# Ten hidden strips by plain products in two passes, in place of eight: a two-layer attention and feed-forward kernel

## The chip, the cores and the metric

One core of a Trainium2 chip runs the whole program in one launch. The metric is the device time in microseconds (us), lower is better. Before the change: 2373.8 us, the median of three runs (2369.51 to 2375.25).

## The reference, cut to what matters

Two attention layers, a pooling mixer and a gated feed-forward block work on 1024 tokens of width 1024, all in float32. The change is in the feed-forward block at the end:

```
def conv_ffn(x, w_in, conv_w, conv_b, w_out):          # x: 1024 tokens x 1024
    h = causal_depthwise_conv(x @ w_in, conv_w, conv_b)  # w_in: 1024 x 5632, 3 taps along the tokens
    val, gate = jnp.split(h, 2, axis=-1)                 # 2816 hidden columns each
    return (jax.nn.silu(gate) * val) @ w_out             # w_out: 2816 x 1024
```

The 2816 hidden columns are 22 strips of 128. The hidden tensor is called u below. It never lies whole on the chip's memory: it goes to DRAM (`ud`) and is fetched for the last matrix product.

## The kernel before, in words

Each factor of a float32 product is split into a high and a low part, so one 128x128 by 128x512 block takes three matmuls (high-high, high-low, low-high). The instructions of all engines come from one list, `steps`: the planner puts steps into it, and each engine's program walks the list in order and issues what is its own. So an engine that waits in one step holds back all of its later steps.

Two ways make the strips of u.

**Plain products by token halves.** `half_task` (line 1475 on) makes one *half*: one strip's value or gate columns for 512 tokens, 8 row tiles x 3 = 24 matmuls into one bank of PSUM (`ffn mm`, lines 1937 to 1939, where a helper records them). `odd_last` (from line 1571) lists the halves: first all strips 0 to 7 for tokens 0 to 511 (the first pass, 16 halves, order `FIRST_PASS`), then all for tokens 512 to 1023 (the second pass, 16 halves, order `SECOND_PASS`). I number the halves 0 to 31 here. After its matmuls a half is left by ScalarE (`half leave`, through the helper of line 2187: the last tap and the bias; in the first pass it also keeps two columns in `TAIL`, in the second it adds them to the first two tokens in three tiny activations) and VectorE adds two taps from PSUM (`half conv`, lines 2749 and 2751). Its bank is free when line 2751 is done. A gate half is then put through silu on ScalarE and multiplied with the value half on VectorE (line 2757). The bank of a half is this:

```
p.bank = (4, 6, 2, 0)[half_no[0] % (3 if n == 0 else 4)]
```

So the first pass goes round three banks and the second, with `half_no` counting on, round four. Strip `TWICE` (6) is last in the first pass and first in the second; its 8 split weight pieces are kept and used again, and `ahead` splits no further than that allows while its first use runs. All other weights are loaded and split for each pass: a piece is 128x256, its high part is made by ScalarE (line 2187), its low part by GpSimd (line 2853); in the second pass every fourth low part goes to VectorE (line 2466). A piece is split 9 pieces ahead of its use, a half uses 4.

One iteration of the planner puts a quarter of a half (one piece, 6 matmuls), then the steps that were deferred from earlier halves, then one step of a side chain. Beside the first pass the side chain is the pooling mixer and the norm of the second token half (`mixed(1)`), and then `turn_sums` (lines 2764, 2770, 2775 on VectorE, with ScalarE's `turn hi`): 28 iterations that make the sums and their splits of the whole normalised input that the block products need. In the kernel before they begin in the first quarter of half 14.

In the second pass the two strips of a pair are brought together (`half_pair`, `pair_sums`): the first-pass results come back from DRAM and VectorE makes four sums (line 2781) in three tiles of X, stored again. The tiles alternate:

```
u.tiles = ((0, 4, 1), (5, 2, 6))[(len(x_parts) - 1) % 2]
```

**Block products.** A unit makes two strips by seven products of blocks each for value and gate together (`product`, lines 2176 to 2178, 12 matmuls of 128x512 each, so 168 for a unit). Their sums of weights (2792), splits of weights (2187, 2786), the adding up of products (2801), taps over 1024 tokens (2807, 2809) and gating (2815) are on VectorE and ScalarE. The first post of a unit goes into tile 0 of X, the second into tile 2. Before the change the 14 remaining strips take 7 units. Six more units of block products make the last matrix product out of u, in three groups of hidden strips (0 to 7, 8 to 15, 16 to 21), and the result is stored. `start_products` is called four halves before the end of the second pass.

Of the kernel before, what the change touches and what calls it, by code (L numbers as in the profile page):

```python
# [27 lines left out]
MEM_UNITS, MEM_RAW = 32, 7  # L28
B_S, B_PT, B_O, B_X = 2, 4, 6, 7
Y_BANKS, X_BANKS, Z_BANKS = ((1, 3), (5, 7)), (4, 6), (2, 0)  # L30
PLAIN = 8
TWICE = 6
FIRST_PASS, SECOND_PASS = (0, 1, 2, 3, 4, 5, 7, 6), (6, 7, 0, 1, 2, 3, 4, 5)
GROUPS = ((0, 4), (8, 4), (16, 3))
A11, A12, A21, A22, ADD = range(5)
SPLIT_OF = (A11, A12, A11, ADD, A21, A12, A22)
# [159 lines left out]
def build(nc, d):  # L196
    ctx = ExitStack()
    with ctx:
        def sb(name, shape, dt=F):
            return ctx.enter_context(nc.sbuf_tensor(name, shape, dt))  # L200
# [27 lines left out]
        SM = sb("SM", [128, 16])  # L228
        SN = sb("SN", [128, 16])
        PSB = sb("PSB", [128, 8])  # L230
        TAIL = sb("TAIL", [128, 16, 2])
        CARRY = sb("CARRY", [128, 8])
        PS = ctx.enter_context(nc.psum_tensor("PS", [128, 8, 512], F))

# [137 lines left out]
        def add_units(us):  # L372
            first, tiles = len(subs), []
            for pieces, kn, n in us:
                per = 256 // n if n <= 256 else 1
                for k in range(0, kn, per):
                    m = min(per, kn - k)
                    subs.append((len(units), k * n, m * n))
                    tiles.append(m)
                units.append(pieces)  # L380
            return first, tiles
# [32 lines left out]
        def ahead(i):  # L414
            while at["split"] < min(i + NSPL - 1 + (4 if at["deep"] else 0), len(subs)):
                no = at["split"]
                split_place(no)
                u = subs[no][0]
                while at["load"] <= min(u + (MEM_RAW if at["load"] < MEM_UNITS else NRAW) - 1, len(units) - 1):
                    load_next()  # L420
                s_whi.add()
                if no < at["both"]:
                    on = s_wlov if no % (2 if no < 2 * MEM_UNITS else 3) else s_wlop
                else:
                    on = s_wlov if at["second"] and no >= at["second"] and no % 4 == 3 else s_wlop
                half_lo.append((on, on.add()))
                put("split", no)
                at["split"] += 1
# [500 lines left out]
        def in_units(w, cols):  # L929
            return [w_cols(w, 0, 4, cols), w_cols(w, 4, 4, cols)]  # L930
# [508 lines left out]
        def pool_task(n, g):  # L1439
            u = pool_first[n, g] = add_units([w_cols(d["pool_w"][g], 0, 2, [(0, 256)])])[0]  # L1440

            def later(c, px):
                yield
                yield
                yield
                yield
                square(ffn[n], c, px)
                squared[n] += 1
                if n == 1:
                    yield  # L1450
                    kept[c] = (d_xt[c], d_xt[c].add(16))
                    put("x spill", c, px)

            def gen():
                ahead(u)
                for o in range(2):
                    c = 2 * g + o
                    bank = at["bank"] % 2
                    at["bank"] += 1
                    pool_no[n, c] = s_pm.add()  # L1460
                    if o == 1:
                        used[u] = used[u + 1] = (s_pm, s_pm.n)
                    put("pool mm", n, g, o, u, bank, s_px.add())
                    defer(later(c, (s_px, s_px.n)))
                    if o == 0:
                        yield
            tasks.append((f"pool{n}{g}", gen, 2))
# [7 lines left out]
        def half_task(j, base, n):  # L1475
            if n == 1 and j == TWICE:
                p = Ffn(j, base, n, *twice[base])
            else:
                p = Ffn(j, base, n, *add_units(in_units(d["ffn_in"], [(base + 128 * j, 128)])))
            if n == 0 and j == TWICE:  # L1480
                twice[base] = (p.first, p.tiles)
# [33 lines left out]
            def gen():  # L1515
# [3 lines left out]
                for i in range(len(p.tiles)):  # L1519
                    ahead(min(p.first + i, twice[0][0] + 1) if n == 0 and j == TWICE else p.first + i)  # L1520
                    if i == len(p.tiles) - 1:
# [49 lines left out]
        def odd_last(first_rest, second_out):  # L1571
            for oc in range(8):
                first_rest(oc)
            for oc in range(8):
                second_out(oc)
                if 2 <= oc < 6:
                    pool_task(0, oc - 2)
            for i in range(2 * PLAIN):
                half_task(FIRST_PASS[i // 2], HID * (i % 2), 0)
                if i in (4, 6, 8, 9):  # L1580
                    pool_task(1, (4, 6, 8, 9).index(i))
            at["second"] = len(subs)
            for i in range(2 * PLAIN):
                half_task(SECOND_PASS[i // 2], HID * (i % 2), 1)

        units_of = [[Quad("in", PLAIN + 2 * u + x, None, u, x) for x in (0, 1)] for u in range((HT_TILES - PLAIN) // 2)]
        for group in GROUPS:
# [4 lines left out]
        for no, p in enumerate(run):  # L1592
            p.no = no
        entered = (HT_TILES - PLAIN) // 2
        wanted = [(m, which) for unit in units_of for m, which in
# [587 lines left out]
        def scalar_program(e):  # L2183
            w = Waits(e)

            def act(out, in_, func=ACT.Copy, **more):
                return e.activation(out, in_, func, **more)  # L2187
# [9 lines left out]
            for kind, *of in steps:  # L2197
# [166 lines left out]
                elif kind == "half leave":  # L2364
# [6 lines left out]
                    if n == 0:  # L2371
                        act(TAIL[:, p.at, :], ps[:, 510:512]).then_inc(s_fa.sem, 1)
                    act(T, ps, ACT.Identity, bias=COL[:, C_CB + col:C_CB + col + 1],
                        scale=COL[:, C_CW + 4 * HT_TILES + col:C_CW + 4 * HT_TILES + col + 1]).then_inc(s_fa.sem, 1)
                    if n == 1:
                        w0, w1 = COL[:, C_CW + col:C_CW + col + 1], COL[:, C_CW + 2 * HT_TILES + col:C_CW + 2 * HT_TILES + col + 1]
                        t0, t1 = TAIL[:, p.at, 0:1], TAIL[:, p.at, 1:2]
                        w.wait_ge(s_fa, p.left - 3)
# [744 lines left out]
```

## Time and profile before, and how to read it

| | |
|---|---|
| median of three runs | 2373.8 us |
| the profiled execution's own time | 2380.02 us |
| its span on the core | 2378.2 us |
| TensorE matmul busy | 2284.0 us, 96% |
| VectorE busy | 1611.1 us, 68% |
| ScalarE busy | 1312.1 us, 55% |
| GpSimd busy | 686.5 us, 29% |
| mean granted TensorE clock | 0.989 |

Engines: PE is TensorE, PEld its weight load, DVE VectorE, ACT ScalarE, POOL GpSimd. A matmul's record covers its whole passage, and the next one starts before it ends, so the rate is read from starts or from counts in a window. On the time axis of the trace the first pass ends at about 1793 us, the second runs from 1801 to 1892, the 7 units of block products for the strips from 1892 to about 2160, and the last matrix product until the end.

### The profile page before, as it was taken

To read this page: it belongs to the slowest core of one execution; us is meant where nothing else is said; L and a number is where in the kernel's file an instruction comes from. 1 tells how busy PE (TensorE), PEld (TensorE's weight loads), DVE (VectorE), ACT (ScalarE), POOL (GpSimd) and SP (SyncE) were. 2 spreads that over 40 slices of the span, in tenths; PEclk is the share of its full clock that TensorE was granted. 3 is DMA by queue.
4 is the path that set the end of the run, shared out by engine and by line. 5 is a ranking of instruction groups with operands and counts; after the bars stand their busy time and mean duration, and the time that the engine had idled before them with its cause. 6 is when DMAs were issued, how large, how long until landed. Compare 5 with 4: busy or idle time off the path is not lost. (4 is left out here: it accounts for less than half of the span.)

```text
span 2378.2 us, 35378 instructions
## 1 busy us (share of the span) xinstructions
PE 2284.0 (96%) x11782; PEld 1939.8 (82%) x11782; DVE 1611.1 (68%) x3297; ACT 1312.1 (55%) x3022; POOL 686.5 (29%) x843
## 2 busy tenths in 40 slices
PE   7999999999999999999999999898998999999999
PEld 6888788888887878888888888786777888887887
DVE  7444676677886433346655566668789788889787
ACT  6444566566775434456656556655555645455532
POOL 3454332311245542222222222555562300000000
PEclk9999999999999999999999999999999999999999
DMA  7322101111243342323232233532352633345734
GB/s 225 117 72 67 40 24 32 32 34 47 61 125 108 94 132 64 93 67 94 85 93 87 77 93 94 188 89 75 88 170 71 201 105 111 113 141 177 229 110 139
DMA packets 331203, 241.68 MB, mean 102 GB/s; under 512 B 66320, under 2 KB 284688, under 8 KB 330512
## 3 DMA queue, kind: packets, MB, share of 16 engines
q1 hardware_dynamic: 331024, 239.42, 33.1%
q8 instruction: 96, 1.57, 0.3%
q14 instruction: 83, 0.68, 0.1%
HBM read 195.59 MB, written 43.78 MB: 101 GB/s over the span
## 5 line engine op out<-in xcount | busy, mean ns | idle before, releaser
L2853 POOL TENSOR_TENSOR WS<-WR,WS 128x256 fp32r<-128x256 f32 x635 | 494.4, 798 | 1027.0 <-ACT WS L2187 1025.0
L1937 PE MATMUL PS<-HT,WS 128*128 128x512 f32 x1492 | 605.6, 406 | 23.5 <-POOL WS L2853 6.5
L1939 PE MATMUL PS<-HT,WS 128*128 128x512 f32 x1492 | 585.9, 393 | 0.0
L1938 PE MATMUL PS<-HT,WS 128*128 128x512 f32 x1492 | 584.6, 392 | 0.0
L1937 PEld LDWEIGHTS PS<-HT,WS 128*128 128x128 f32 x1492 | 282.9, 190 | 83.9 <-issue 15.1
L1939 PEld LDWEIGHTS PS<-HT,WS 128*128 128x128 f32 x1492 | 282.1, 189 | 62.1
L1938 PEld LDWEIGHTS PS<-HT,WS 128*128 128x128 f32 x1492 | 283.5, 190 | 52.2
L2187 ACT ACTIVATE PT<-PS 128x512 fp32r<-128x512 f32 x352 | 185.7, 528 | 208.5 <-PE PS L2050 208.2
L2187 ACT ACTIVATE WS<-WR 128x256 fp32r<-128x256 f32 x658 | 245.7, 410 | 89.2 <-PE PS L1939 61.8
L2435 DVE TENSOR_TENSOR PT<-PS,PT 128x512 fp32r<-128x512 f32 x352 | 211.4, 609 | 94.0 <-ACT PT L2187 91.6
L2083 PE MATMUL PS<-PT,QKV 128*128 128x256 f32 (+1 forms) x1248 | 209.3, 289 | 3.2 <-DVE YB L2614 2.4
L2187 ACT ACTIVATE QKV<-PS 64x512 fp32r<-64x512 f32 (+2 forms) x208 | 121.6, 585 | 140.5 <-PE PS L1939 122.0
L2083 PEld LDWEIGHTS PS<-PT,QKV 128*128 128x128 f32 x1248 | 180.5, 192 | 10.5 <-ACT PT L2187 3.8
L2050 PE MATMUL PS<-ID,PY 128*128 128x128 f32 x1072 | 184.1, 275 | 0.1
L2436 DVE SCALAR_TENSOR_TENSOR QKV<-PS,QKV 64x512 fp32r<-64x512 f32 (+1 forms) x112 | 77.2, 689 | 113.8 <-ACT QKV L2187 111.6
L2187 ACT ACTIVATE PY<-PY,ST 128x384 f32<-128x384 f32 (+1 forms) x192 | 115.6, 602 | 37.5 <-DVE ST L2565 25.5
L2037 PE MATMUL PS<-QKV 128*128 128x384 f32 (+2 forms) x320 | 121.7, 381 | 14.5 <-ACT PY L2187 13.0
L2558 DVE CUSTOM_DVE_ANT_0 PY<-PS,EO 128x384 f32<-128x384 f32 (+1 forms) x192 | 103.5, 539 | 42.3 <-PE PS L2038 41.6
L2050 PEld LDWEIGHTS PS<-ID,PY 128*128 128x128 f32 x1072 | 128.1, 141 | 0.6 <-ACT PY L2187 0.4
L2435 DVE TENSOR_TENSOR QKV<-PS,QKV 64x512 fp32r<-64x512 f32 (+2 forms) x96 | 63.9, 666 | 93.6 <-ACT QKV L2187 92.3
L2545 DVE TENSOR_REDUCE ST<-PS 128x1 f32<-128x256 f32 (+1 forms) x128 | 102.3, 819 | 35.9 <-PE PS L2025 20.9
L2187 ACT ACTIVATE HT<-EO 128x512 fp32r<-128x512 f32 x112 | 70.1, 628 | 93.1 <-PE PS L2178 30.1
(286 smaller groups left out, 4594.8 us busy)
## 6 DMA issues: line engine op xcount, KB each, us to landing
WR<-in_w_in_odd SPq DMA_DIRECT2D x106, 256.0 KB, 2.9
EO<-in_grid SPq DMA_DIRECT2D x48, 384.0 KB, 3.1
WR<-in_ffn_in SPq DMA_DIRECT2D x60, 256.0 KB, 2.9
WR<-in_w_in_even SPq DMA_DIRECT2D x100, 128.0 KB, 2.6
WR<-in_w_out_odd SPq DMA_DIRECT2D x48, 256.0 KB, 2.8
yd<-PY SPq DMA_DIRECT2D x44, 256.0 KB, 3.3
EO<-in_ffn_in SPq DMA_DIRECT2D x35, 256.0 KB, 3.1
WR<-in_w_in_even SPq DMA_DIRECT2D x34, 256.0 KB, 2.9
```

What stands on the lines that cost most here:

```text
L1937: e.matmul(out, wh, rh, start=start, stop=False)
L1938: e.matmul(out, wh, rl, start=False, stop=False)
L1939: return e.matmul(out, wl, rh, start=False, stop=stop)
L2037: e.matmul(out, q, kh, start=True, stop=False)
L2050: m = e.transpose(PS[:, B_PT + pb, o + 128 * z:o + 128 * z + 128], p_at(job.c, job.scores[x].slot, p0, p0 + 128), ID[:, :])
L2083: m = e.matmul(out, vv, p, start=a, stop=b)
L2187: return e.activation(out, in_, func, **more)
L2435: return e.tensor_tensor(out, src, f32(hi), ALU.subtract)
L2436: return e.scalar_tensor_tensor(out=out, in0=src, scalar=scale, in1=f32(hi), op0=ALU.mult, op1=ALU.subtract)
L2545: e.tensor_reduce(st[:, 1:2], src, AX.XY, ALU.max, negate=True).then_inc(s_mx.sem, 1)
L2558: e.tensor_tensor_reduce(out=two_parts(p, s.cut), in0=src, in1=two_parts(bias, s.cut), scale=1.0, scalar=NEG, op0=ALU.add, op1=ALU.max, ac ...
L2853: e.tensor_tensor(ws(i, 1, n), RAW[raw_slot(u)][:, o:o + n], f32(ws(i, 0, n)), ALU.subtract).then_inc(s_wlop.sem, 1)
```

## The change

The number of plain strips goes from 8 to 10, the strip with kept weights from 6 to 8, the two orders get two more strips, and `TAIL` gets 20 rows. Nothing else is edited. So the passes have 20 halves each (0 to 39), six units of block products make the remaining 12 strips, and every position that is counted from the start of the first pass (the pooling products after its entries 4, 6, 8, 9; the side chain) stays where it was.

```
-PLAIN = 8
-TWICE = 6
-FIRST_PASS, SECOND_PASS = (0, 1, 2, 3, 4, 5, 7, 6), (6, 7, 0, 1, 2, 3, 4, 5)
+PLAIN = 10
+TWICE = 8
+FIRST_PASS, SECOND_PASS = (0, 1, 2, 3, 4, 5, 6, 7, 9, 8), (8, 9, 0, 1, 2, 3, 4, 5, 6, 7)
...
-        TAIL = sb("TAIL", [128, 16, 2])
+        TAIL = sb("TAIL", [128, 2 * PLAIN, 2])
```

## Rows read from the trace of the kernel before

**Rows 1.** Windows: length, then busy (x instructions) of PE, PEld, DVE, ACT, POOL; clock; DMA.

```profile
1640.00:1800.00 160.00, 146.75 (x646) 119.30 (x644) 130.36 (x188) 84.37 (x191) 89.23 (x97) 0.96 0.37 117
...
1812.00:1843.00 31.00, 31.00 (x138) 25.47 (x137) 30.69 (x45) 19.48 (x48) 12.89 (x15) 1.00 0.29 85
...
1847.30:1891.80 44.50, 44.50 (x197) 36.75 (x197) 30.24 (x43) 28.70 (x74) 17.75 (x22) 1.00 0.81 246
1892.00:2154.00 262.00, 261.33 (x1152) 215.88 (x1152) 224.85 (x302) 137.44 (x211) 0.00 (x0) 1.00 0.37 116
1910.00:2150.00 240.00, 240.00 (x1060) 198.82 (x1059) 203.32 (x267) 127.28 (x191) 0.00 (x0) 1.00 0.37 116
```

**Rows 2.** Waits of PE, 1600 to 1910 us: total us, times, longest.

```profile
PE PS L1937 <- DVE SG L2751: 7.7, 1, 7.7
...
PE PS L1937 <- DVE PT L2466: 0.7, 1, 0.7
PE PS L2176 <- ACT X L2187: 0.7, 1, 0.7
```

**Rows 3.** Timeline of PE: start us, us, engine, line; idle before and releaser.

```profile
1792.96 0.39 PE L1939 MATMUL PS<-HT,WS 128*128 128x512 f32 x1
1801.02 0.80 PE L1937 MATMUL PS<-HT,PT 128*128 128x512 f32 x1 [7.67 <-DVE SG L2751]
1801.61 0.63 PE L1938 MATMUL PS<-HT,PT 128*128 128x512 f32 x1
...
1807.04 0.40 PE L1939 MATMUL PS<-HT,WS 128*128 128x512 f32 x1
```

**Rows 4.** Timeline of DVE: the taps of halves 14 to 19.

```profile
1795.11 0.75 DVE L2751 SCALAR_TENSOR_TENSOR SG<-PS,COL,SG 128x510 f32<-128x510 f32 x1
...
1800.22 0.75 DVE L2751 SCALAR_TENSOR_TENSOR SG<-PS,COL,SG 128x510 f32<-128x510 f32 x1
...
1811.36 0.75 DVE L2749 SCALAR_TENSOR_TENSOR PY<-PS,COL,PY 128x511 f32<-128x511 f32 x1 [3.50 <-ACT PY L2187]
...
1818.23 0.75 DVE L2751 SCALAR_TENSOR_TENSOR PY<-PS,COL,PY 128x510 f32<-128x510 f32 x1
...
1826.75 0.75 DVE L2751 SCALAR_TENSOR_TENSOR SG<-PS,COL,SG 128x510 f32<-128x510 f32 x1
...
1833.33 0.75 DVE L2751 SCALAR_TENSOR_TENSOR SG<-PS,COL,SG 128x510 f32<-128x510 f32 x1
```

**Rows 5.** Groups of DVE: the first from 1789.6 to 1801, the others 1812 to 1843.

```profile
L2770 DVE TENSOR_TENSOR EO<-EO 128x512 f32<-128x512 f32 x4 | 2.8, 688 | 0.1
...
L2775 DVE TENSOR_TENSOR QKV<-PY,QKV 128x512 fp32r<-128x512 f32 x6 | 4.5, 772 | 0.0
L2770 DVE TENSOR_TENSOR PY<-PY 128x512 f32<-128x512 f32 x5 | 4.0, 802 | 0.1
L2775 DVE TENSOR_TENSOR QKV<-EO,QKV 128x512 fp32r<-128x512 f32 x4 | 3.5, 904 | 0.0
...
L2466 DVE TENSOR_TENSOR WS<-WR,WS 128x256 fp32r<-128x256 f32 x3 | 1.2, 415 | 0.0
...
L2757 DVE TENSOR_TENSOR SG<-SG 128x512 f32<-128x512 f32 x1 | 1.2, 1225 | 0.0
L2757 DVE TENSOR_TENSOR PY<-PY 128x512 f32<-128x512 f32 x1 | 1.2, 1223 | 0.0
```

**Rows 6.** Timeline of POOL around the end of the first pass.

```profile
1787.41 1.44 POOL L2853 TENSOR_TENSOR PT<-WR,PT 128x256 fp32r<-128x256 f32 x2 [0.28 <-ACT PT L2187]
1804.54 1.17 POOL L2853 TENSOR_TENSOR PT<-WR,PT 128x256 fp32r<-128x256 f32 x1 [15.70 <-ACT PT L2187]
```

**Rows 7.** Timeline of ACT where the block products begin.

```profile
1902.90 0.57 ACT L2187 ACTIVATE X<-PS 128x512 f32<-128x512 f32 x1
...
1906.00 0.60 ACT L2187 ACTIVATE X<-PS 128x512 f32<-128x512 f32 x1 [2.01 <-DMA ud<-X]
```

**Rows 8.** Timeline of DVE there: the last sum of the last plain pair.

```profile
1903.60 0.69 DVE L2781 TENSOR_TENSOR X<-X 128x512 f32<-128x512 f32 x1
```

## The prediction

> **What bounds the kernel now.** I read the windows first. The profile's mean would call TensorE the bound, but the stages differ. In the block products it takes a matmul every 240 / 1060 = 0.226 us with no idle time, and VectorE has 37 us of 240 to spare; in the second pass it takes one every 44.5 / 197 = 0.226 us, with VectorE at 30.24 of 44.5. From 1640 to 1800 us TensorE fits in 646 instructions where 160 us would hold some 700, and from 1812 to 1843 us VectorE is busy for 30.69 of 31 us [rows 1]. So matmuls are the price wherever VectorE keeps up, and around the change from the first pass to the second VectorE sets the pace.
>
> Then the waits of TensorE: between 1600 and 1910 us one wait is the longest, 7.7 us on line 2751, the taps that free a bank [rows 2]. The timeline shows its place: the last matmul of half 15 starts at 1792.96, the first of half 16 at 1801.02; and then the clock: steps of 0.427 us from 1801.61 until 1807.04, 13 of them, where 0.227 is usual, so it ran at 1.2 GHz instead of 2.4 after 7.67 us of idleness [rows 3]. Half 15 has bank 15 mod 3 = 0, half 16 bank 16 mod 4 = 0 of the same list: half 16 waits for its direct predecessor's taps, which end at 1800.22 + 0.75 = 1800.97 [rows 4].
>
> **Matmuls.** The change adds 8 halves, 8 x 24 = 192 matmuls, and removes one unit of 168. Net 24 x 0.227 = **+5.4 us**, on the path, as both stages run at the matmul rate [rows 1].
>
> **The stall between the passes.** The first pass now ends with half 19 (bank 19 mod 3 = 1, bank 6), and half 20 takes bank 4, last used by half 18. There is one half of 5.45 us in between, which looks like the end of the stall. But the 28 steps of turn sums still begin at half 14, so they now all fall beside first-pass halves, and the taps of half 18 queue behind some 20 of them. When are these done? Before, they ended at 1826.75 + 0.75 = 1827.5 [rows 4]. Take away what had delayed VectorE there: 3.50 us in which it waited for half 16 [rows 4], and three low parts of line 2466, each 0.41 long and about 0.33 from start to start [rows 5], which only the second pass has. That gives 1823.0. TensorE without a stall ends half 19 at 1793.2 + 4 x 5.45 = 1815.0 and then waits 8.0 us: the same stall, one half later in relation to its bank, because four more halves let VectorE fall back further. With 2.85 us for the slow clock (13 x 0.2, and 0.25 for the first step) half 21 starts at 1823.0 + 5.45 + 2.85 = 1831.3; before it was at 1801.02 + 5 x 5.45 + 2.85 = 1831.1. Half 21 needs bank 6, free when half 19's taps end, (1833.33 + 0.75) - 3.50 - 4 x 0.33 = 1829.3: no second wait. Term: **+0.2 us**.
>
> **GpSimd beside the sums.** While the kept strip ran, GpSimd had nothing: 15.70 us idle before 1804.54 [rows 6]. Now strips 7 and 9 follow half 14 and their weights go on being split. By the planner's rule of 9 pieces ahead, 16 low parts come to GpSimd before the taps of half 18 are put, where it had 7. VectorE's operations with two inputs in SBUF take 688 ns while GpSimd is idle; with 15 GpSimd instructions about [rows 1] they take 772, 802 and 904 ns on average and 1.22 us singly. The excess is 6 x 0.084 + 5 x 0.114 + 4 x 0.216 + 2 x 0.54 = 3.0 us, 0.2 for each GpSimd instruction [rows 5]. Nine more: **+1.8 us**, at the place where VectorE has no slack. Bounds: 0, if they fall beside operations that read PSUM, to 9 x 0.54 = 4.9.
>
> A rule of the Trainium skill speaks here against the change. "SBUF — State Buffer", section "SBUF: two separate sides", says that VectorE with two SBUF inputs and GpSimd lock one port pair for a whole instruction, and the other blocks. The doubled durations agree; full blocking each time would put the sum near the upper bound.
>
> **Smaller edits.** The wait of 0.7 us on line 2466 in the second pass [rows 2] came from VectorE's arrears; the sums will be over before: **-0.7 us** (bounds -0.7 and 0). The last plain pair is now the fifth, so its sums lie in tiles 0, 4, 1 instead of 5, 2, 6. The unit's first post writes tile 0. It began at 1902.90 [rows 7] and must now follow the pair's last sum, over at 1903.60 + 0.69 = 1904.29 [rows 8]: +1.4, and the next product's wait for the store of tile 2 (2.01 us of ScalarE [rows 7]) goes, which gives back 0.3. **+1.1 us** (bounds 0 and 3, if tile 1's store comes late, though its post is six products off). What TensorE waited there already, 0.7 [rows 2], stays.
>
> At nothing: eight more halves' taps, silu and products on VectorE and ScalarE (VectorE 68% busy in the second pass [rows 1]; in the first they are the queue costed above); 16 weight loads of 256 KB more against 8 fewer, two pairs of stores and fetches more, all on SyncE's queue, with the DMA engines at 0.81 but no wait of TensorE in that stretch [rows 1]. If that cover failed, TensorE would wait for pieces. ScalarE's splits now stand behind turn steps that wait for VectorE; the piece is 9 quarters, 12 us, ahead, and up to 8 us of such waiting vanish in the stall at half 20 anyway.
>
> **Sum:** 5.4 + 0.2 + 1.8 - 0.7 + 1.1 = +7.8 us. The profiled execution's own time, 2380.02, would become 2387.8; it stands 6.2 above the median of the runs, and on the median 2373.8 the forecast is **2381.6 us**, +0.33%. The measurement can tell about 0.3%, 7.1 us, so this lies just past it.
>
> **The rivals.** *The lag is absorbed* (the other side). If VectorE ends half 18's taps by 1815.0, bank 4 is free in time, no stall and no slow clock: 5.4 - (8.06 - 0.23 + 2.85 = 10.7) - 0.7 + 1.1 = -4.9, 2368.9. For it: nothing waits for a direct predecessor any more. Against: 8 us of VectorE work would have to vanish, and it is shown back to back [rows 1, 4]. Chance 0.17, a third of it past -7.1 with some luck elsewhere.
> *GpSimd costs nothing*: the forecast without 1.8, +6.0, 2379.8. VectorE's operations of lines 2764 and 2751 read PSUM and were not lengthened. Chance 0.2, mostly within 0.3%.
> *Full collisions*: every added low part doubles an operation, 4.9 in place of 1.8: +10.9, 2384.7. Chance 0.12. That is the skill's rule with bad luck.
> *Weights late*: pieces for halves 14 to 19 come more than 8 us late, or a fetch holds a pair, 4 us on top: 2386. Against: no wait of TensorE is for a load [rows 2]. Chance 0.06.
> The forecast has 0.45, itself uncertain by 2.5 us: 2379 to 2384, two thirds of it slower.
>
> **Numbers.** Slower: 0.30 + 0.05 + 0.12 + 0.05 = 0.52. Faster: 0.06, and 0.02 for what I don't see, 0.08. Within 0.3%: 0.40. The range reaches from 2370, near the absorbed lag, to 2387, past the late weights.
>
> **What would show it.** Matmuls: 1152 fewer by 168 in the block stage, 8 x 24 more before. Stall: TensorE's longest wait still on line 2751, 7 to 11 us, before half 20, with slow steps after it; if it is under 2 us I am wrong and the lag was absorbed. GpSimd: idle time of some 15 us moved behind half 17, and lines 2770 and 2775 longer beside halves 14 to 17. Tiles: the wait before the fifth block product near 2 us, released by the post into X. The forecast is wrong if VectorE shows gaps between the taps of halves 16 and 18.

## The result, and the profile after

The changed kernel takes 2379.11 us (median of 12 runs, 2376.58 to 2385.75), the one before beside it 2373.28 (12 runs, 2369.51 to 2380.11): ratio 1.003, 95% interval 1.0019 to 1.0040, so 0.3% slower. Run once more against the kernel before (`ten_again` below) the ratio was 1.0014, interval 1.0001 to 1.0027. The two together say slower by 0.14 to 0.3%, some 3 to 7 us. The forecast was 2381.6, +0.33%.

The first part of the page of the kernel after:

```profile
span 2383.8 us, 35528 instructions
## 1 busy us (share of the span) xinstructions
PE 2287.6 (96%) x11806; PEld 1943.3 (82%) x11806; DVE 1598.9 (67%) x3283; ACT 1316.3 (55%) x3054; POOL 705.8 (30%) x871
```

TensorE has 11806 matmuls where it had 11782: 24 more, as counted, while VectorE has less to do than before (1611.1 us then). Where TensorE sets the pace, these extra matmuls are a cost that no schedule hides.

The spans of single executions are a poor measure here, so I set a common point: the transposes of line 2132, which prepare the turn sums in the first quarter ahead of half 14. Up to it both programs issue the same instructions. TensorE's timeline of the kernel before at this point, at the first matmuls of half 21, of the block products and of the last matrix product, and at the last matmul:

```profile
1781.85 0.38 PE L2132 MATMUL PS<-ID,SN 128*128 128x128 f32 x2
...
1831.12 0.39 PE L1937 MATMUL PS<-HT,PT 128*128 128x512 f32 x1
...
1892.05 0.39 PE L2176 MATMUL PS<-HT,WS 128*128 128x512 f32 x1
...
2164.25 0.39 PE L2176 MATMUL PS<-HT 128*128 128x512 f32 x1
...
2374.66 0.39 PE L2178 MATMUL PS<-QKV,WS 128*128 128x512 f32 x1
```

The same places in the kernel after:

```profile
1783.93 0.27 PE L2132 MATMUL PS<-ID,SN 128*128 128x128 f32 x1
...
1833.50 0.39 PE L1937 MATMUL PS<-HT,PT 128*128 128x512 f32 x1
...
1936.86 0.39 PE L2176 MATMUL PS<-HT,WS 128*128 128x512 f32 x1
...
2169.26 0.39 PE L2176 MATMUL PS<-HT,WS 128*128 128x512 f32 x1
...
2380.24 0.39 PE L2178 MATMUL PS<-QKV,HT 128*128 128x512 f32 x1
```

| from | to | before, us | after, us | difference |
|---|---|---|---|---|
| common point | half 21 | 49.27 | 49.57 | +0.3 |
| half 21 | block products | 60.93 | 103.36 | +42.4 |
| block products | last matrix product | 272.20 | 232.40 | -39.8 |
| last matrix product | last matmul | 210.41 | 210.98 | +0.6 |
| common point | last matmul | 592.81 | 596.31 | +3.5 |

The other 2.1 us of the difference between the two spans lie ahead of the common point. Two of the rows hold a piece of chance that cancels in the sum: after a wait of 2.62 us just before the last matrix product, matmuls came at the half rate in this profile of before and not in that of after. This makes the third difference 0.5 us more negative and the fourth 0.6 us more positive; from that wait to the last matmul it is 217.54 us before and 217.56 after.

The waits of TensorE in the kernel after, 1785 to 1936 us, answer to [rows 2]:

```profile
PE PS L1937 <- DVE SG L2751: 6.5, 1, 6.5
PE PS L1937 <- POOL PT L2853: 1.4, 2, 0.8
PE PS L1937 <- DVE PY L2751: 0.4, 1, 0.4
```

The wait of line 2466 and the one at the entry of the block products are gone; the one on line 2751 is there again. Its place in TensorE's timeline, against [rows 3]:

```profile
1819.44 0.39 PE L1939 MATMUL PS<-HT,WS 128*128 128x512 f32 x1
1826.31 0.80 PE L1937 MATMUL PS<-HT,WS 128*128 128x512 f32 x1 [6.48 <-DVE SG L2751]
1826.90 0.63 PE L1938 MATMUL PS<-HT,WS 128*128 128x512 f32 x1
...
1829.85 0.39 PE L1939 MATMUL PS<-HT,WS 128*128 128x512 f32 x1
```

The taps that released it are those of half 18, as the timeline of VectorE shows (against [rows 4]):

```profile
1825.51 0.75 DVE L2751 SCALAR_TENSOR_TENSOR SG<-PS,COL,SG 128x510 f32<-128x510 f32 x1
```

They end at 1826.26, TensorE goes on at 1826.31. The two windows below are the same stretch, 8 to 42 us after the common point, before and after (columns as in [rows 1]). GpSimd has 16 instructions where it had 7, and VectorE goes from instruction to instruction without a wait:

```profile
1789.80:1823.80 34.00, 26.33 (x104) 21.25 (x103) 30.12 (x45) 15.76 (x35) 6.36 (x7) 0.85 0.18 54
```

```profile
1791.90:1825.90 34.00, 26.13 (x112) 20.35 (x110) 33.58 (x47) 17.36 (x41) 12.75 (x16) 0.96 0.29 89
```

### The profile page after: what moved, and what is told of

It reads as the page before. It is cut to its first block and busy times, and to the rows that moved or that the text cites. A ratio compares the mean times of both kernels' runs of the same rounds, so it can differ in the third digit from the quotient of the medians.

```text
span 2383.8 us, 35528 instructions
## 1 busy us (share of the span) xinstructions
PE 2287.6 (96%) x11806; PEld 1943.3 (82%) x11806; DVE 1598.9 (67%) x3283; ACT 1316.3 (55%) x3054; POOL 705.8 (30%) x871
## 5 line engine op out<-in xcount | busy, mean ns | idle before, releaser
L2853 POOL TENSOR_TENSOR WS<-WR,WS 128x256 fp32r<-128x256 f32 x652 | 506.2, 796 | 1051.9 <-ACT WS L2187 1050.8
L1937 PE MATMUL PS<-HT,WS 128*128 128x512 f32 x1528 | 619.0, 405 | 29.7 <-DVE SG L2751 6.5
L1939 PE MATMUL PS<-HT,WS 128*128 128x512 f32 x1528 | 600.0, 393 | 0.0
L1938 PE MATMUL PS<-HT,WS 128*128 128x512 f32 x1528 | 598.6, 392 | 0.0
L1937 PEld LDWEIGHTS PS<-HT,WS 128*128 128x128 f32 x1528 | 289.5, 189 | 91.2 <-issue 12.0
L1939 PEld LDWEIGHTS PS<-HT,WS 128*128 128x128 f32 x1528 | 288.8, 189 | 63.4
L1938 PEld LDWEIGHTS PS<-HT,WS 128*128 128x128 f32 x1528 | 289.9, 190 | 53.6
L2187 ACT ACTIVATE WS<-WR 128x256 fp32r<-128x256 f32 x678 | 252.9, 409 | 96.0 <-PE PS L1939 62.6
L2037 PE MATMUL PS<-QKV 128*128 128x384 f32 (+2 forms) x320 | 122.8, 384 | 13.3 <-ACT PY L2187 13.1
L2038 PE MATMUL PS<-QKV 128*128 128x384 f32 (+2 forms) x320 | 115.9, 363 | 0.0
```

The source lines that it names most:

```text
L1937: e.matmul(out, wh, rh, start=start, stop=False)
L1938: e.matmul(out, wh, rl, start=False, stop=False)
L1939: return e.matmul(out, wl, rh, start=False, stop=stop)
L2037: e.matmul(out, q, kh, start=True, stop=False)
L2853: e.tensor_tensor(ws(i, 1, n), RAW[raw_slot(u)][:, o:o + n], f32(ws(i, 0, n)), ALU.subtract).then_inc(s_wlop.sem, 1)
```

## The experiments

"From the common point" is always the time to the last matmul's start in the profile of that kernel. Ratios are to the kernel before in the same session.

**1. The size of TAIL alone** (`tail_only`), in the kernel before:

```
-        TAIL = sb("TAIL", [128, 16, 2])
+        TAIL = sb("TAIL", [128, 20, 2])
```

> The kernel before with TAIL at 20 rows and nothing else. The two profiles differ by 2.1 us already where the turn sums begin, though their programs are the same up to there. Theory A, chance: the same time as before within 0.3%, ratio 0.999 to 1.001. Theory B, the larger TAIL moves what lies behind it and costs 2 us somewhere: ratio 1.0008 or more with an interval above 1, and the difference to be seen again in the profile ahead of 1780 us.

Measured: ratio 0.9986, interval 0.9974 to 0.9998; 593.9 us from the common point, 1.1 more than before (of two executions that differ in nothing that the engines do). So the larger TAIL costs nothing, and Theory B falls. That its interval lies just under 1 shows how far two sets of runs of practically one program drift apart: 0.1% is not to be read from such ratios, nor 1 us from the time after the common point in single profiles.

**2. The changed kernel again** (`ten_again`).

> The changed kernel unchanged, beside the runs of before on this chip. Counted from the point where the turn sums are prepared to the last matmul, its profile was 3.5 us longer than the one of before, the medians 5.8. Theory A, the rest is chance of the runs: ratio 1.000 to 1.003, and the same 3.5 (3 to 4) from that point in the profile. Theory B, ten strips also slow down what comes before that point: ratio 1.0025 or more and the point again later than 1781.8 us.

Ratio 1.0014, interval 1.0001 to 1.0027, and 597.2 us from the common point. The common point itself was at 1773.8 us, 10 us earlier than in the first profile of the same program. So what comes before it is chance, and Theory B falls. The 597.2 is 4.4 more than the 592.8 of before, a little over the 3 to 4 of Theory A; against the 593.9 of `tail_only`, which is as good a "before", it is 3.3. The stall is the same in both profiles of ten strips (half 20 starts 42.38 and 42.40 us after the common point); what differs is how many matmuls ran at the half rate after it (6 and 10).

**3. Four banks from half 10 on**, with ten strips (`ten_banks`) and with eight (`eight_banks`):

```
-                p.bank = (4, 6, 2, 0)[half_no[0] % (3 if n == 0 else 4)]
+                p.bank = (4, 6, 2)[half_no[0] % 3] if half_no[0] < 10 else (2, 4, 0, 6)[half_no[0] % 4]
```

> Ten strips, and from half 10 on four banks in turn in both passes (bank 0 is out of use by then) in place of three in the first pass. Theory A, the wait of 6.5 us before half 20 is VectorE's arrears meeting a bank that was used two halves before: with four banks half 20 needs the taps of half 16 only, done 7 us before TensorE is there, so the wait and the half-rate matmuls after it go, and the small waits of halves 18 and 19: 8 to 10 us faster than ten strips, 2369 to 2371, ratio to before 0.998 to 0.9995. Theory B, VectorE is the bound from half 14 to 20 and the wait only moves to half 22 or 24: ratio 1.001 to 1.003, with a wait of 4 us or more on line 2751 later on.

> The kernel before with the same four banks from half 10 on. Theory A: its wait of 7.7 us before half 16 goes, and the slow clock after it, 10.7 us together; the turn sums now reach half 21 with VectorE further behind (it was 12 us behind at half 20 with the stall, so up to 18 without it, against three halves, 16.4 us, that four banks allow), so 1 to 4 us come back: 2364 to 2367, ratio 0.9955 to 0.998. Theory B, the same work of VectorE must be done anyway: ratio 0.999 to 1.001.

Ten: ratio 1.0001 (0.9992 to 1.0011), 592.5 us from the common point, 3.8 less than without. Eight: 0.9988 (0.9977 to 0.9998), 589.1, 3.7 less. The wait on line 2751 is gone in both, but less than half of the time came back. TensorE's waits with eight strips, 1780 to 1880 us, show why:

```profile
PE PS L1937 <- POOL WS L2853: 2.9, 3, 1.6
PE PS L1937 <- DVE PT L2466: 1.2, 2, 0.7
PE PS L1937 <- DVE WS L2466: 0.9, 1, 0.9
PE PS L1937 <- POOL PT L2853: 0.8, 1, 0.8
```

and with ten, 1777 to 1930 us:

```profile
PE PS L1937 <- POOL WS L2853: 2.7, 1, 2.7
PE PS L1937 <- POOL PT L2853: 1.9, 2, 1.2
```

TensorE now waits for low parts of weights. Both ratios lie outside the range that Theory A gave (0.998 to 0.9995 with ten, 0.9955 to 0.998 with eight), eight strips come just below the 0.999 to 1.001 of Theory B, and the later wait on line 2751 that Theory B had for ten strips did not come. The bank was only the first of two limits that VectorE's arrears set. ScalarE shows the second: it makes the high parts of weights, and in its queue they stand behind steps of the turn sums that wait for VectorE. Its waits with eight strips, 1786 to 1832 us:

```profile
ACT QKV L2187 <- DVE PY L2770: 9.9, 5, 2.8
ACT QKV L2187 <- DVE EO L2770: 9.5, 5, 2.6
```

A low part is made from its high part, so GpSimd gets it late as well.

**4. Twelve strips** (`twelve`): PLAIN 12, TWICE 10, the orders longer by two, TAIL in the place of PCT.

> Twelve strips (TAIL lies in the place of PCT, which is read no more by then). Against ten: another 24 matmuls net, +5.4 us. Theory A, the stall is the turn sums ending just at the change of pass: they end at half 20 as before, now four halves ahead of the change, VectorE has 10 us to catch up, and half 24 (bank 4) needs half 21's taps: no wait of over 1 us there, though a wait of 1 to 3 us may come at half 19 to 21, still on three banks with VectorE 11 us behind. Without the 6.5 us and the slow clock of 1.7: 2373 to 2378, ratio to before 1.000 to 1.002. Theory B, a change of pass costs its stall whatever surrounds it: 2384 to 2386, ratio 1.0045 or more.

Ratio 1.0026 (1.0016 to 1.0036), 599.3 us from the common point: 3.0 more than ten. The one long wait at the change of pass is gone, as Theory A had it. The time is not what Theory A gave (ratio 1.000 to 1.002): 5.4 us for matmuls less the 8.2 of the stall would have made it 2.8 faster than ten. In place of the stall there are more of the shorter waits, 5.8 us where ten strips have 1.8, and with what they bring after them TensorE loses 8.6 us up to the block products where it loses 11.0 with ten (both against halves of 5.44 us without a wait, as in `ten_spread` below). The waits, 1779 to 1970 us:

```profile
PE PS L1937 <- POOL WS L2853: 2.5, 3, 1.6
PE PS L1937 <- POOL PT L2853: 1.5, 2, 0.8
PE PS L1937 <- DVE SG L2751: 1.3, 2, 0.8
PE PS L1937 <- DVE PY L2751: 0.5, 2, 0.4
```

So a change of pass has no long stall of its own; in these runs it is the turn sums that hold TensorE back, at the change of pass or ahead of it.

**5. The turn sums at half the rate**, with ten strips (`ten_spread`), with eight (`eight_spread`), and together with the four banks (`eight_banks_spread`, `ten_banks_spread`), written so or to the same effect:

```
-                yield from turn_sums()
+                for _ in turn_sums():
+                    yield
+                    yield
```

> Ten strips, three banks, one step of the turn sums in every second iteration in place of every one, so that they run beside halves 14 to 28. Theory A, VectorE's arrears are the rate of the turn sums (8 us of them per 5.45 us half-and-a-bit): at the change of pass VectorE is less than a half behind, no wait of over 1.5 us before half 20, no slow clock, and no waits for GpSimd's low parts, whose ScalarE halves stood behind turn steps: from the common point 585 to 589 us (596.3 with ten, 592.8 before), ratio 0.996 to 0.999. Theory B, the work is the same, so the wait moves into the second pass and to the start of the block products: from the common point 592 or more.

> The kernel before with the turn sums in every second iteration and its three banks in the first pass kept, so that half 16 still takes the bank of half 15. Theory A, bank and arrears both make the stall: VectorE is less behind, but the direct predecessor's taps are never done in time: a wait of 2 to 5 us before half 16 in place of 7.7, and 585 to 588 us from the common point. Theory B, the arrears alone make it: under 1 us, 582. Theory C, the bank alone: still 7 us.

> Eight strips, four banks from half 10 on, the turn sums in every second iteration. Theory A: no stall between the passes and none for weights, 581 to 584 us from the common point, ratio 0.994 to 0.997, faster than both kernels. Theory B: with eight strips the sums now reach the last halves of the second pass, where VectorE and ScalarE also make the first weights of the block products, and the time comes back there: 588 or more from the common point.

> Ten strips with both repairs, four banks from half 10 and the turn sums in every second iteration; beside eight strips with both (581.5 us from the common point) and ten with the spread sums alone (585.3). Theory A, without stalls on either side two more plain strips cost their 24 matmuls, 5.4 us, less what the start of the block products costs with eight (1.3 us of waits there): 585 to 587 from the common point, the fourth bank adding nothing once the sums are spread; ratio to before 0.996 to 0.999. Theory B, ten strips have something for them that the stall had hidden: 583 or less.

| kernel | ratio to before | 95% interval | from the common point |
|---|---|---|---|
| ten_spread | 0.9977 | 0.9965 to 0.9989 | 585.3 |
| eight_spread | 0.9974 | 0.9959 to 0.9989 | 587.9 |
| ten_banks_spread | 0.9978 | 0.9963 to 0.9992 | 585.3 |
| eight_banks_spread | 0.9959 | 0.9946 to 0.9973 | 581.5 |

The windows of `ten_spread` through the rest of the two passes:

```profile
1790.00:1830.00 40.00, 40.00 (x178) 33.14 (x177) 35.92 (x51) 23.16 (x57) 17.56 (x21) 1.00 0.35 107
1830.00:1870.00 40.00, 40.00 (x178) 33.10 (x178) 37.37 (x54) 27.46 (x69) 19.01 (x23) 1.00 0.53 168
1870.00:1910.00 40.00, 40.00 (x178) 33.14 (x177) 23.23 (x33) 24.83 (x63) 16.70 (x21) 1.00 0.69 208
```

TensorE has no idle time at all, with the same work and the same three banks in the first pass; VectorE keeps 4.1 and 2.6 us of 40 free in the first two windows, where it had nothing to spare in the change as made. With eight strips and three banks one wait stays (1779 to 1884 us; two inserted lines move 1937 to 1939 and 2751 to 2753):

```profile
PE PS L1939 <- DVE SG L2753: 5.4, 1, 5.4
```

Half 16 takes the bank of half 15, and a direct predecessor's taps are late even when VectorE is not behind: 5.4 us, above the 2 to 5 that I had expected. VectorE itself waits 0.17 us ahead of these taps, for ScalarE. The last matmul of half 15 starts at 1789.3, ScalarE begins to leave the half only at 1792.7, after 2.80 us of waiting for a sum that stands before it in its queue. Ten strips don't have this wait: their half 20 takes the bank of half 18. This is what ten strips really bring, and in the change as made it doesn't show, because the sums eat it.

With both repairs on both sides ten strips are 3.9 us slower than eight (585.33 - 581.45), against 5.4 for their matmuls; the fourth bank adds nothing to ten strips with spread sums. The best version is eight strips with both repairs: 0.4% faster than the kernel before, and by these single profiles faster than ten strips (the two ratios come from different sessions and their intervals overlap). With the spread sums alone, eight and ten strips can't be told apart by their ratios.

**6. The tiles of the last pair** (`ten_tiles`):

```
-                    u.tiles = ((0, 4, 1), (5, 2, 6))[(len(x_parts) - 1) % 2]
+                    u.tiles = ((5, 2, 6), (0, 4, 1))[(len(x_parts) - 1) % 2]
```

> Ten strips with the two sets of tiles exchanged, so that the last plain pair uses 5, 2, 6 as before and tile 0 is free when the block products begin. The prediction put 1.1 us on this. Theory A, the wait of ScalarE for the pair's last sum (1.4 us in the profile of ten) goes, but TensorE did not wait for it: the same time from the common point as ten, 596.3 within 0.7. Theory B: 595.2 or less, as predicted.

596.3 us from the common point in one execution, the same as ten strips: Theory A. ScalarE's waits at the entry of the block products, first ten strips (1937 to 1950 us), then with the tiles exchanged (1930 to 1950 us):

```profile
ACT X L2187 <- DVE X L2781: 1.4, 1, 1.4
```

```profile
ACT X L2187 <- DMA ud<-X: 2.0, 1, 2.0
```

One wait takes the place of the other, and TensorE has none in either.

**7. More of GpSimd beside the sums** (`ten_pool`): at each turn sum GpSimd also runs

```
+                    e.tensor_tensor(RW[:, :], RW[:, :], RW[:, :], ALU.mult).then_inc(s_extra.sem, 1)
```

> Ten strips, and GpSimd multiplies a 128x256 scratch tile with itself beside each of the 16 sums of the turn steps: 16 more GpSimd instructions with inputs in SBUF, whose product nothing uses. The prediction priced one at 0.2 us of VectorE's time where VectorE has no slack; the profile of ten had 16 low parts where before had 9, and the excess of VectorE's two-input operations rose by only 0.4 us. Theory A, 0.2 each: some 13 of them lie before the taps of half 18, the second pass starts 2.5 us later (45 us after the common point in place of 42.4). Theory B, 0.05 each: 43.1 or less. Theory C, a full lock each time, 0.54: 49.

The second pass starts 45.3 us after the common point in place of 42.4. Twelve of the added instructions lie before the taps of half 18, and VectorE has no wait there, so 2.9 / 12 = 0.24 us for one: Theory A. The whole, from the common point: 600.1. This is one execution, but the start of the second pass hardly scatters: 42.38, 42.40 and 42.39 us in the three profiles of ten strips with the sums as they were.

## Why the prediction was right

The direction and the mechanism came out as argued, and the time lies in the range; single terms did not come out, and the sum was about twice what the profiles show from the common point.

**Matmuls, +5.4.** Confirmed: 24 more on the page, half 21 to the block products takes 19 halves in 103.36 us, 5.44 each, without a wait.

**The stall returns one half later.** Confirmed in place and cause: before half 20, released by half 18's taps. The text had these at 1823.0 on the clock of the kernel before, 41.15 us after the common point, and 42.95 with GpSimd's share; they came 42.33 after it. Two further checks hold too: no second wait at half 21, and the arrears behind it (`ten_spread` removes the stall by the rate of the sums alone). One doesn't: the wait was to be 7 to 11 us long and was 6.48. TensorE was put at half 20 after 33.15 us without a stall, and was there after 35.9, mostly because it had already waited three times, 1.8 us together, in halves 18 and 19. The prediction had no such waits; as the taps set the end, they only shorten the long one.

**GpSimd, +1.8: a size off.** The added instructions of experiment 7 cost 0.24 each, near the 0.2 of the prediction. But the nine that the change adds delayed the taps by 42.33 - 41.15 = 1.2 us, 0.13 each. VectorE's own records agree: up to these taps four of its two-input operations were lengthened before, by 2.0 us together, and seven after, by 3.3 us. The step that failed is the multiplication: that an added low part meets a two-input operation as often as those did from which the price was read. GpSimd's long idle time moved as forecast: it is 13.82 us now, before 1835.01.

**The slow clock, 2.85.** Mis-sized: 6 steps at the half rate after 6.48 us of idleness, not 13, so half 20 took 7.19 us from its first matmul to half 21's first, where 8.3 was forecast. With the taps 0.6 earlier this makes +0.3 to half 21 in place of +2.0. This term is the one that chance moves: in `ten_again` half 20 took 8.00 us, and in `tail_only` half 16 took 7.71 where it took 8.35 in the profile of before, so for another pair of profiles the +0.3 could be some +1.7.

**Line 2466, -0.7.** Confirmed, the wait is gone. All in all the eleven halves of the second pass behind half 20 had taken 60.93 us before, 1.1 more than at 5.44 each.

**Tiles, +1.1: wrong.** ScalarE does wait 1.4 us for the pair's last sum, but its post is in time all the same: 9.60 us after the first matmul of the block products, where before it came after 10.85 (1902.90 - 1892.05).

```profile
1946.46 0.60 ACT L2187 ACTIVATE X<-PS 128x512 f32<-128x512 f32 x1 [1.42 <-DVE X L2781]
```

The step that failed took the first post's position relative to TensorE from the kernel before, where ScalarE and VectorE entered the block products late. That they were later there than in the kernel after is seen in two places. The last half's taps end 1899.49 + 0.75 - 1892.05 = 8.2 us after TensorE has gone on to the block products before, and 5.4 us after. And ScalarE's waits for loads of weights, 1850 to 1905 us before and 1895 to 1950 us after:

```profile
ACT PT L2187 <- DMA WR<-in_ffn_in: 6.5, 1, 6.5
```

```profile
ACT WS L2187 <- DMA WR<-in_ffn_in: 3.8, 1, 3.8
```

Why a load came 2.7 us less late with ten strips was not tried; that the four halves between the sums and that place let the queues catch up is a guess. So why the entry is earlier stays open. From the first matmul of the block products to the wait of 2.62 us at their end it is 265.07 us before and 225.82 after; a unit of 168 matmuls is 38.07 (the difference between `twelve` and ten strips over the same stretch), so the entry gained 1.2 us instead of losing 1.1. The gain depends on the execution of before: in `tail_only` the same stretch takes 266.54.

**The sum** was 7.8; with the terms as measured it is 5.4 + 0.3 - 1.1 - 1.2 = 3.4. From the common point two executions show 3.5 and 4.4, while the medians say 5.8 and 2.4. That the first medians came as near as 5.8 to 7.8 is in part luck. "Slower by over 0.3%" was put at 0.52 and "within 0.3%" at 0.40; the measured 0.3% (0.19 to 0.40) and 0.14% (0.01 to 0.27) don't support the first over the second, and the 0.40 deserved to be the larger.

**The rivals.** That the lag is absorbed did not happen, and experiment 5 shows what it would have needed: sums at half the rate. "Weights late" had been given 0.06 as a cost on top; it was the hidden second limit, 1.4 us already in the changed kernel, within its stall, and the first to appear when the bank was no longer in the way.

## What to carry to other kernels

When a stall sits where a buffer is reused at once, ask first how far behind the releasing engine is, and whether the change gives it time or only gives it more before the same place; here four more halves beside the sums moved the arrears with them. Removing one wait (the bank) shows the next one that the same arrears feed (the weights). Halving the rate of the side work removed both with ten strips, 11.0 us, and was worth more than the bank (3.8) or the number of strips; with eight strips it brought 4.9, and one wait on the bank stayed. Compare single profiles from a point up to which the programs are the same, not by their spans.

## What the runs showed of the hardware that I had not expected

The half clock after a wait does not depend on the wait alone. After 6.48 and 6.49 us of idleness at the same place of the same program, 6 and 10 steps came at 0.427 us; the kernel before had 12 after 7.67 us. Of the very program of before, with only the size of TAIL changed (`tail_only`), a profile had 9 after the same 7.67 us. The wait of 2.6 us late in the block products was followed by 5 to 8 slow steps in five of the thirteen profiles (7 in that of before) and by none in the other eight, `tail_only` among them. There it cost nothing: where the steps were not slow, TensorE waited 0.7 us more for VectorE a few steps later, and from this wait to the last matmul all thirteen take 217.5 to 217.6 us.

Nine profiles of programs that are alike up to the common point reach it between 1773.8 and 1783.9 us: 10 us of chance ahead of a change worth 4. The scatter goes together with the granted clock: of the 29 executions of the kernel before beside `ten_again`, the fastest took 2369.49 us at a mean clock of 0.994 and the slowest 2383.69 at 0.986. What makes the clock differ was not tried.
